# A fourth quad in seven products in the gate/up blocks of a float32 encoder trunk

## The reference

```
h = rmsnorm(x, norm_ffn[l])
x = x + (jax.nn.silu(h @ w_gate[l]) * (h @ w_up[l])) @ w_down[l]
```

## Time and profile before

| | |
|---|---|
| median of 3 runs | 2180.6 us (2180.28 to 2180.61) |
| the profiled execution | 2180.93 us, its span 2179.1 us |
| granted TensorE clock | 0.999 |
| PE busy | 2167.8 us, 99% of the span |
| DVE busy | 1728.6 us, 79% |
| ACT busy | 1202.9 us, 55% |
| POOL busy | 209.3 us, 10% |
| the chain that ended last | PE 96%, DVE 1%, ACT 1% |

### The profile page before, as it was taken

The page is one execution under the profiler, slowest core; times in us unless marked ns, Lnnn a source line. Parts: engine busy times, 40 slices in busy tenths (PEclk is TensorE's granted clock), DMA queues, the critical chain, the costliest instruction groups (busy, mean ns, idle before and its releaser), DMA issues.

```text
span 2179.1 us, 27606 instructions
## 1 busy us (share of the span) xinstructions
PE 2167.8 (99%) x10481; PEld 1808.6 (83%) x10481; DVE 1728.6 (79%) x2139; ACT 1202.9 (55%) x1646; POOL 209.3 (10%) x246
## 2 busy tenths in 40 slices
PE   9999999999999999999999999999999999999998
PEld 7888888888888888888888888888888888888886
DVE  6776676888889887788866667768988888888887
ACT  6445554655556555555544555546655555555554
POOL 0031120100000000000001311200000000000000
PEclk9999999999999999999999999999999999999999
DMA  9655455756775675667666544557567567756674
GB/s 346 208 175 173 173 171 177 224 187 207 245 224 188 221 237 193 204 223 218 224 213 202 178 163 167 181 174 223 189 230 233 194 203 244 224 182 224 213 217 179
DMA packets 131556, 449.42 MB, mean 206 GB/s; under 512 B 15072, under 2 KB 15712, under 8 KB 131040
## 3 DMA queue, kind: packets, MB, share of 16 engines
q1 hardware_dynamic: 115344, 416.40, 53.9%
q0 software_dynamic: 14784, 28.32, 7.6%
q10 hardware_dynamic: 1296, 2.94, 0.4%
HBM read 441.31 MB, written 2.10 MB: 203 GB/s over the span
## 4 chain that ended last, share of the span: by engine, by line
PE 96%; DVE 1%; ACT 1%; issue 0%; POOL 0%; DMA 0%; SPq 0%; ACTq 0%; DVEq 0%
PE bank L1674 18%; PE bank L1676 18%; PE bank L1675 18%; PE bank L1648 14%; PE bank L1651 7%; PE bank L1686 7%; PE bank L1688 7%; PE bank L1687 7%; PE bank L1839 1%; PE bank L1798 1%; PE bank L1821 1%; DVE wlo L1025 0%; PE bank L1777 0%; POOL o_rms L560 0%; PE bank L1807 0%
## 5 line engine op out<-in xcount | busy, mean ns | idle before, releaser
L628 ACT ACTIVATE whi<-raw 128x1024 fp32r<-128x1024 f32 x596 | 625.7, 1060 | 469.2 <-PE bank L1676 285.8
L1018 DVE TENSOR_TENSOR wlo<-raw,whi 128x1024 fp32r<-128x1024 f32 x596 | 724.5, 1232 | 180.9 <-ACT whi L628 167.5
L634 ACT ACTIVATE whi<-raw 128x1024 fp32r<-128x1024 f32 x368 | 343.1, 950 | 234.2 <-PE bank L1676 176.4
L1025 DVE TENSOR_TENSOR wlo<-raw,whi 128x1024 fp32r<-128x1024 f32 x368 | 390.4, 1088 | 77.1 <-ACT whi L634 75.9
L1648 PE MATMUL bank<-xg,whi 128*128 128x512 f32 x1280 | 407.0, 399 | 0.2 <-DVE wlo L1249 0.2
L1674 PE MATMUL bank<-whi,xg 128*128 128x512 f32 x1024 | 402.7, 393 | 0.0
L1676 PE MATMUL bank<-whi,xg 128*128 128x512 f32 x1024 | 399.1, 390 | 0.0
L1675 PE MATMUL bank<-wlo,xg 128*128 128x512 f32 x1024 | 398.9, 390 | 0.0
L1651 PEld LDWEIGHTS bank<-xg,wlo 128*128 128x128 f32 x1280 | 240.4, 188 | 56.9
L1651 PE MATMUL bank<-xg,wlo 128*128 128x256 f32 x1280 | 252.1, 278 | 0.0
L1676 PEld LDWEIGHTS bank<-whi,xg 128*128 128x128 f32 x1024 | 192.2, 188 | 40.3
(11 more groups left out here) (159 smaller groups left out, 2767.8 us busy)
## 6 DMA issues: line engine op xcount, KB each, us to landing
raw<-w_gu_dram SPq DMA_DIRECT2D x352, 512.0 KB, 5.2
raw<-w_in_dram SPq DMA_DIRECT2D x188, 512.0 KB, 4.5
raw<-w_down_dram SPq DMA_DIRECT2D x176, 512.0 KB, 5.3
raw<-w_out_dram SPq DMA_DIRECT2D x64, 512.0 KB, 4.4
raw<-w_gu_dram POOLq DMA_DIRECT2D x64, 256.0 KB, 6.1
raw<-w_down_dram POOLq DMA_DIRECT2D x28, 256.0 KB, 4.2
swapped<-qk POOLq DMA_DIRECT2D x32, 128.0 KB, 2.7
x_t<-x_t_dram SPq DMA_DIRECT2D x8, 256.0 KB, 6.7
```

The source lines that it names most:

```text
L628: act.activation(whi[:, blk.slot(k)], raw[:, slot, half * UNIT_KT:(half + 1) * UNIT_KT, :], ACT.Copy).then_inc(hi_ready, 1)
L634: act.activation(whi[:, quad.slot(n), 0:tiles.stop - tiles.start], raw[:, quad.raw(), tiles, :], ACT.Copy).then_inc(hi_ready, 1)
L1018: dve.tensor_tensor(wlo[:, blk.slot(k)], raw[:, slot, half * UNIT_KT:(half + 1) * UNIT_KT, :], lo_bits(whi[:, blk.slot(k)]), ALU.subtract) ...
L1025: dve.tensor_tensor(wlo[:, quad.slot(n), into], raw[:, quad.raw(), tiles, :], lo_bits(whi[:, quad.slot(n), into]), ALU.subtract).then_inc( ...
```

## The change

GU_SEVENS goes from 3 to 4: in each of the first 10 pairs of a layer unit 3 of the two blocks becomes a fourth quad, and units 4 to 7 stay plain. The forms of gate/up get a second batch of two quads in place of one. The orders of all engines are written anew around the four quads, and the head of DVE gets an order of its own, in which `gates_ups` of the left block's second half comes one split earlier and the last split comes behind `hidden_products`. POOL's loop is written in another form and issues one add more per pair, in the order of the quads. The sums stay where they were: b + h by POOL's DMA, the three others on DVE. The eleventh pair and the down blocks keep their orders.

```diff
-GU_SEVENS = 3
+GU_SEVENS = 4
-GU_ORDER = [("left", 3), ("left", 4), ("right", 3), ("right", 4), ("first", 0), ("first", 1), ("second", 0),
-            ("first", 2), ("left", 5), ("right", 5), ("second", 1), ("second", 2),
-            ("left", 6), ("left", 7), ("right", 6), ("right", 7)]
+GU_ORDER = [("left", 4), ("left", 5), ("right", 4), ("right", 5), ("first", 0), ("first", 1), ("second", 0),
+            ("first", 2), ("second", 1), ("left", 6), ("right", 6), ("first", 3), ("second", 2), ("second", 3),
+            ("left", 7), ("right", 7)]
...
-               "gu": [(shared_end - 4 * FORM, shared_end - 2 * FORM, 2), (shared_end - 6 * FORM, shared_end - 5 * FORM, 1)]}
+               "gu": [(shared_end - 4 * FORM, shared_end - 2 * FORM, 2), (shared_end - 8 * FORM, shared_end - 6 * FORM, 2)]}
...
+            def add_four(quads):
+                for k in range(1, 4):
+                    add_b(quads[k])
...
-            def gu_three(pair, prior=None):
+            def gu_four(pair, prior=None):
...
                 first_parts(q2)
-                split(left, 5, 6)
-                split(right, 5, 6)
                 second_parts(q1)
+                split(left, 6, 7)
+                split(right, 6, 7)
+                first_parts(q3)
                 second_parts(q2)
+                second_parts(q3)
...
+            def four_head(prior, pair):
+                split(left, 4, 5)
+                gates_ups(prior, 0, 1)
+                split(left, 5, 6)
+                hidden_products(layer, g, 0)
+                hidden_products(layer, g, 1)
+                gates_ups(prior, 1, 0)
+                gates_ups(prior, 1, 1)
+                split(right, 4, 5)
+                hidden_products(layer, h, 0)
+                hidden_products(layer, h, 1)
+                split(right, 5, 6)
...
+                split_quad(q0, 0, slice(0, 2))
+                    hidden_low(prior.layer, prior.blocks[0].i)
+                first_sum(q0)
+                split_quad(q0, 1, slice(2, 3))
+                    hidden_low(prior.layer, prior.blocks[1].i)
+                split_quad(q1, 0, slice(0, 2))
+                first_sum(q1)
+                second_sum(q0)
+                third_sum(q0)
+                split_quad(q1, 1, slice(2, 3))
+                second_parts(q0)
+                split_quad(q2, 0, slice(0, 2))
+                second_sum(q1)
+                third_sum(q1)
+                split_quad(q2, 1, slice(2, 3))
+                second_parts(q1)
+                split(left, 6, 7)
+                first_sum(q2)
+                split(right, 6, 7)
+                split_quad(q3, 0, slice(0, 2))
+                second_sum(q2)
+                third_sum(q2)
+                first_sum(q3)
+                split_quad(q3, 1, slice(2, 3))
+                second_sum(q3)
+                third_sum(q3)
+                second_parts(q2)
+                second_parts(q3)
...
-            def gu_three(pair):
+            def gu_four(pair):
                 first_products(pair.quads[0])
                 first_products(pair.quads[1])
                 second_products(pair.quads[0])
                 first_products(pair.quads[2])
-                plain(left, 5)
-                plain(right, 5)
                 second_products(pair.quads[1])
+                plain(left, 6)
+                plain(right, 6)
+                first_products(pair.quads[3])
                 second_products(pair.quads[2])
+                second_products(pair.quads[3])
```

More of the change, by code:

```diff
@@ L410, in build_program @@
     first_sums = sem("first_sums")
+    third_sums = sem("third_sums")
     second_sums = sem("second_sums")
-    third_sums = sem("third_sums")
     form_step = sem("form_step")
@@ L599, in _ @@
                 rms(2 * layer + 1)
[L600 to L606, removed]
+                add_four(plan.pairs[layer, "gu", 0].quads)
+                for p in range(1, NGU // 2 - 1):
+                    add_b(plan.pairs[layer, "gu", p].quads[0])
+                    add_four(plan.pairs[layer, "gu", p].quads)
+                for pair in (plan.pairs[layer, "gu", NGU // 2 - 1], *(plan.pairs[layer, "down", p] for p in range(2))):
+                    for quad in pair.quads.values():
                         add_b(quad)
@@ L741, in hidden_out, with four_tail, two_tail @@
                 act.activation(hidden[:, 2 * g:2 * g + 2, 0:S], hidden_bank(g), ACT.Copy).then_inc(hidden_hi, 1)
-            def gu_tail(pair):
+            def four_tail(pair):
+                left, right = pair.blocks
+                split(left, 7, 8)
+                split(right, 7, 8)
+                sum_out(pair)
+            def two_tail(pair):
                 left, right = pair.blocks
@@ L761, in gu_head @@
                 silu(layer, right, 1)
-            def gu_three(pair, prior=None):
+            def gu_four(pair, prior=None):
                 left, right = pair.blocks
-                q0, q1, q2 = (pair.quads[k] for k in range(3))
+                q0, q1, q2, q3 = (pair.quads[k] for k in range(4))
                 act.wait_ge(raw_landed[q0.raw()][0], q0.landed())
@@ L944, in _ @@
                 left, right = pair.blocks
-                split(left, 3, 5)
+                split(left, 4, 6)
                 squares(ffn, NCH - 1)
-                split(right, 3, 5)
+                split(right, 4, 6)
                 normed(ffn, NCH - 1)
-                gu_three(pair)
-                gu_tail(pair)
+                gu_four(pair)
+                four_tail(pair)
                 for p in range(1, NGU // 2 - 1):
@@ L953, in _ @@
                     left, right = pair.blocks
-                    gu_head(prior, ((left, 3), (left, 4), (right, 3), (right, 4)))
-                    gu_three(pair, prior)
-                    gu_tail(pair)
+                    gu_head(prior, ((left, 4), (left, 5), (right, 4), (right, 5)))
+                    gu_four(pair, prior)
+                    four_tail(pair)
                 prior, pair = pair, plan.pairs[layer, "gu", NGU // 2 - 1]
@@ L960, in _ @@
                 gu_two(pair, prior)
-                gu_tail(pair)
+                two_tail(pair)
                 prior, pair = pair, plan.pairs[layer, "down", 0]
@@ L1121, in gates_ups, with four_tail, two_tail @@
                                   ).then_inc(bank_free, 1)
-            def gu_tail(pair):
+            def four_tail(pair):
+                left, right = pair.blocks
+                split(left, 7, 8)
+                split(right, 7, 8)
+                gu_fold(pair)
+                gates_ups(pair, 0, 0)
+            def two_tail(pair):
                 left, right = pair.blocks
@@ L1145, in gu_head, with gu_four @@
                 hidden_products(layer, right, 1)
-            def gu_three(pair, prior=None):
+            def four_head(prior, pair):
+                layer = prior.layer
+                g, h = (b.i for b in prior.blocks)
                 left, right = pair.blocks
-                q0, q1, q2 = (pair.quads[k] for k in range(3))
+                split(left, 4, 5)
[9 more added lines that the diff above has]
+                split(right, 5, 6)
+            def gu_four(pair, prior=None):
+                left, right = pair.blocks
+                q0, q1, q2, q3 = (pair.quads[k] for k in range(4))
                 split_quad(q0, 0, slice(0, 2))
@@ L1550, in _ @@
                     left, right = pair.blocks
-                    gu_head(prior, ((left, 3), (left, 4), (right, 3), (right, 4)))
-                    gu_three(pair, prior)
-                    gu_tail(pair)
+                    four_head(prior, pair)
+                    gu_four(pair, prior)
+                    four_tail(pair)
                 prior, pair = pair, plan.pairs[layer, "gu", NGU // 2 - 1]
@@ L1863, in gu_two, with four_tail, two_tail @@
                 second_products(pair.quads[1])
-            def gu_tail(pair):
+            def four_tail(pair):
+                for blk in pair.blocks:
+                    plain(blk, 7)
+            def two_tail(pair):
                 for blk in pair.blocks:
@@ L1971, in _ @@
                 normed_there(ffn, 5)
-                plain(left, 3)
                 plain(left, 4)
+                plain(left, 5)
                 turn_x(ffn, NCH - 1)
-                plain(right, 3)
                 plain(right, 4)
-                gu_three(pair)
-                gu_tail(pair)
+                plain(right, 5)
+                gu_four(pair)
+                four_tail(pair)
                 for p in range(1, NGU // 2 - 1):
@@ L1981, in _ @@
                     left, right = pair.blocks
-                    plain(left, 3)
+                    plain(left, 4)
                     turn_hidden(layer, 2 * p - 2)
-                    plain(left, 4)
+                    plain(left, 5)
                     turn_hidden(layer, 2 * p - 1)
-                    plain(right, 3)
                     plain(right, 4)
-                    gu_three(pair)
-                    gu_tail(pair)
```

(3 more changed lines are left out.)

9 lines of the change are left out of this document (removed).

## The result

The changed kernel takes 2212.7 us (median of 4 runs, 2210.4 to 2216.0) against 2180.5 (4 runs) of the kernel before on the same chip: ratio 1.0149, 95% interval 1.0136 to 1.0162, 32 us slower. The forecast was 2202, the range 2176 to 2216. The profiled execution after is the slowest of its four, 2216.0 us, 3.3 above the median; its span is 2214.2 us, 35.1 more than the one before.

A forecast was written before the change was run, and what follows sets the result against it. PE, busy 99%, was taken to bound the kernel. Per pair 1.68 us late minus 0.68 saved gives +1.00; x 20 is +20.0, with forms +21.2; on 2180.9 that makes 2202 us, range 2176 to 2216.

The forecast's parts named there:

- The mechanism: In each changed pair, fourth quad's add lands late beside units 7's loads; DVE waits, PE 1.68 us late, net +1.00 us.
- the working: Step-by-step times from a pair's first product to the third quad's second half: add issued at 10.35, DVE waits 1.5 us.
- PE's two stops: PE idle about 1.7 us a pair, before the third quad's second half and a little before the second quad's.
- The term of the add: POOL's DMA for the fourth quad's b + h, issued at 10.35 us of the stretch, taken as 6.5 us long.
- 20 x 1.68: PE's lateness at the third quad's third part, 1.68 us in each of the 20 changed pairs, before the matmul saving.
- The add is in time: Rival: fourth quad's add up to 5.05 us is not waited for; -8.8 us in all, 2172; chance 0.13.
- 0.18 us late at the third quad: With no wait for the add, DVE's chain alone readies the third quad's third part at 19.22; -0.50 us a pair.
- break-even for the add: Fourth quad's add length, 5.4 us, at which the change is worth nothing; below 5.2 it is measurably faster.
- The rule that the prediction took from the Trainium skill: Rival "DVE holds up POOL": two-port DVE operations lock GpSimd's descriptor writing; 24 us more, 2226; chance 0.03.
- The second add: Rival: the add for the next pair's first quad is late too; each pair loses one us more, 2222; chance 0.09.
- The small terms: ACT's extra copies, under 2.1 us a pair, hidden; POOL's extra add unqueued; forms 1.2 us in two layers.

The follow-up runs named there:

- e1: The changed kernel without the fourth quad's b + h add and the waits for it (that part not computed): 2182.7 us, ratio 1.0009 to the kernel before.
- e2: The changed kernel, full computation, with SP issuing the loads of units 7 only when the fourth quad's add has landed: 2182.9 us, ratio 1.0010.
- e9: e6 with the second quad's second sum moved well ahead of its split, and without SP's wait on the loads of units 7: 2201.4 us, ratio 1.0093.
- e6: e5 with POOL's second add ahead of the norm's power and the second batch's form sums behind unit 6's split: 2184.0 us, ratio 1.0015.
- e5: e2 with the second quad's third sum moved ahead of the first quad's second parts in DVE's order: 2187.6 us, ratio 1.0032.
- e7: The kernel before with only the larger second batch of forms (two quads, the fourth's forms unused): 2182.2 us against 2180.7, ratio 1.0007.

## Why the prediction was right, and where it was too small

**The mechanism stands.** The fourth quad's add is issued with the loads of units 7 and lands too late, DVE waits, PE waits for DVE: shown by e1 (without the add), e2 (without the loads beside it), and e9 (with them again). In the pair shown: DVE's wait 1.49 us, 1.5 in the working; the add issued 5.2 us after SP's first load, 5.25 in the working; PE's two stops where they were named.

**The term of the add** was 6.5 us a pair; the fourth adds of the 20 pairs took 5.3 to 8.1, mean 6.75, 6.4 in the first layer and 7.1 in the second. That would be +0.25 x 20 = 5 us. By the waits themselves it is less: 33.2 us in the 20 pairs against 30 in the working, so 3.2. The 6.5 came from two single rows, 5.9 and 7.5, and the mean lies about midway. Two things in its working were wrong and did not show in it, so that it came so near is partly luck. The landing times of the earlier trace rows are of all 92 adds of line 572, 28 of them of w_down; the page of the profile before has 6.1 us as the median of the 64 adds of gate/up, not 5.8, and the shortest of these took 4.2, not 4.0. And the working had the loads run beside the whole of the add, while most of what they cost it comes before its first packet.

**What the sum left out.** I counted every start of a matmul in the gate/up stages against PE's step of 0.2267. Long gaps sum to 38.4 us after and 1.6 before: 36.8 more, where the prediction had 20 x 1.68 = 33.6. Short ones (a step of 0.25 to 0.34) sum to 12.7 against 5.7: 7.1 more, and 0 in the prediction. Some 5 of these are PE's restart: the matmul after a stop takes 0.50 and the next starts 0.34 later in place of 0.23 (727.44 to 727.78 above). Each stop costs 0.11 us beyond itself, and two a pair came newly. The rest is mostly one more step of 0.31 a pair beside the transposes, three in place of two, with no stop in it. Then 1.4 us in which the clock was low, 2.0 in steps a little over the regular one, 1.3 ahead of the two stages, where the forms are, and -13.6 for the matmuls saved: 35.0 in all. The spans of the two profiled executions differ by 35.1. The medians differ by 32.2; the other three executions left no profile, so which of these terms was smaller in them is not known. Their mean granted clock was 0.999 against 0.998 in the profiled one, which fits that they had no stretch at the lower clock.

**The rival that fell short.** "The add is in time" was put at 2172. e1 and e2 are that case, and they took 2183. So the DVE chain had been priced some 10 us too cheaply: it gave 0.18 us late at the third quad, though the working's own times (7.90 + 1.23 and a handover of 0.05 against 39 matmuls, 8.84) make the second quad's third part 0.34 late, which comes first and then decides. Measured, with the restart of that stop and the step beside the transposes, a pair is 42.45, not 42.07: 7.6 of the 11. The rest lies in the first pair of each layer, where the prediction took no extra cost: e2 still has three PE stops of 0.17 to 0.41 us there, and e6 took 3.7 us off e5 there and in the output block. The prediction's break-even for the add, 5.4 us, therefore doesn't exist: with no add at all (e1) this order was not faster than before (ratio 1.0009).

**The Trainium skill** (DMA: Bandwidth & Descriptors, Anatomy of one DMA — SWDGE (gpsimd) path) gives 2.0 us and bytes over 436 GB/s, by which 2.6 us for 256 KB is an estimate. The shortest of all adds in e2 took 3.8, and 4.0 is the mean of the 20 with no load beside them, so the trace disagrees. In the Trainium skill (DMA: Bandwidth & Descriptors, SWDGE vs HWDGE vs iDMA) it is said that DMAs of POOL and of SP go into different queues inside each DMA engine, and that the engine round-robins between them. The trace agrees for the last 3.2 us of the add at 716.89, in which both queues have packets under way (43 and 50% of the engines' time). It doesn't explain the 1.6 us by which the add's first packet came later than in e2. The rule that the prediction took from the Trainium skill (SBUF — State Buffer, SBUF: two separate sides) is of DVE operations in a two-port mode, and no row shows that the operations here, nearly all of them TENSOR_TENSOR, run in one. At 93% DVE the issue takes 865 ns in the median, 1190 at most (862 and 1187 before): no sign of it. And in e2, with the same work on DVE, the first packet of each fourth add comes 1.6 us after its issue, so it isn't DVE that makes it 3.4. Nothing came of this rival.

**The second add** (the next pair's first quad, 0.09) did not come: of DVE's 22 waits for an add, none is for the first quad's add of a following pair; the pair from 690.02 waits for one add only, the fourth quad's.

**The small terms.** ACT 26.1 us a pair (24.8 + 1.3); nothing queued in POOL; forms 1.5 us by e7, and 1.4 by its trace (twice 0.61 + 0.11), where 1.2 in all stood: the difference is the restart.

## What to carry to other kernels

When an engine order has little slack, follow each new dependency over all its engines, DMA included, to the point where it is wanted, and note what the same queue slot releases at that instant: the transfer that decides is lengthened by the one that you release beside it. Holding back a load that is not urgent was worth 26 to 30 us here, more than the 13.6 of matmuls that the change set out to save. In this kernel a saving of 0.68 us a pair on a full PE was eaten by one stop of 0.3 us, its restart of 0.11 and some short steps, so the saving counts only once the short stops are gone.

## What the runs showed that I had not expected

**The clock.** In one pair of the changed kernel PE stopped for 0.43 and, 2 us later, 1.50 us. Then its matmuls came at 0.43 us in place of 0.23 for 3.4 us; these are windows before, in and after:

```profile
1737.00:1739.20 2.20, 0.70 (x4) 0.27 (x2) 2.20 (x4) 1.79 (x2) 0.00 (x0) 1.00 0.00 0
1739.20:1742.60 3.40, 3.40 (x8) 2.64 (x9) 3.27 (x3) 0.75 (x2) 0.00 (x0) 0.50 0.34 90
1742.60:1745.00 2.40, 2.40 (x12) 1.99 (x11) 1.32 (x2) 1.58 (x2) 0.00 (x0) 0.99 1.01 405
```

The granted clock is 0.50, the lower of its two levels (1.2 of 2.4 GHz). That pair took 46.57 us. Two other pairs, with stops of 0.70 and 1.50 us, kept the full clock and took 45.3 to 45.5; a fourth pair had a stop of 1.50 and kept it as well. e9 has two such dips, each of 3.4 us behind a stop of 1.5, out of four such stops. So a stall can cost more than its length, but not always does, and what decides was not tried.

**Cheap work can be a cover, and a small gap a small place.** In e5 a sum of 0.6 us was moved forward. Where it had stood it had covered the time between a sum and the split that needs ACT's copy of it, so taking it away gained nothing there. Where it went, the gap was 0.35 us, and the rest made PE late: the kernel was 4.7 us slower. A neighbour that looks like load on the bottleneck can be what hides a latency, and an idle stretch of an engine holds only work that is no longer than it.

**Two layers, one code, two lengths.** The fourth add is 0.7 us longer in the second layer, in the same place of the order. Half of this is three adds of 7.7 to 8.1 us, in the pairs from 1700.53 on and in every second one after it; the other seven take 6.5 to 7.0. In e9 the long adds of that layer (6.8 to 7.5) come in every second pair too. Why was not tried.
